# Where the softmax probabilities are scaled in a diffusion backbone step: on VectorE, or on ScalarE ahead of the recurrent roots

## What is computed

```python
s = jnp.einsum('bqgrd,bkgd->bgrqk', q, k) * (HEAD_DIM ** -0.5)
p = jax.nn.softmax(jnp.concatenate([s, sink_col], axis=-1), axis=-1)[..., :-1]
out = jnp.einsum('bgrqk,bkgd->bqgrd', p, v)
```

```python
u = jnp.sqrt(-jnp.expm1(2.0 * log_a)) * (i * xc)     # h = exp(log_a) * h + u
```

## Time and profile before

| | |
|---|---|
| median of 3 runs | 1509.36 us (1505.26 to 1509.89) |
| the profiled execution | 1510.04 us; its span, first to last instruction, is 1508.2 us |
| mean granted TensorE clock | 0.992 |
| busy, PE / DVE / ACT / POOL | 1448.1 / 1152.2 / 865.7 / 214.3 us |
| L1717, probabilities times reciprocal | 48 instructions, 285 to 423 ns |
| L1255, table loads and square roots | 16 loads of 1283 ns; 32 roots of 508 to 532 ns |

### The profile page before, as it was taken

One profiled execution on the slowest core, in us unless ns is written; L12 is line 12 of the kernel. 1 busy time (PEld: TensorE's weight loads), 2 busy tenths in 40 slices (PEclk: granted clock), 3 DMA queues, 4 the chain that ended last, 5 costly groups with the idle time before them and its releaser, 6 DMA issues.

```text
span 1508.2 us, 20056 instructions
## 1 busy us (share of the span) xinstructions
PE 1448.1 (96%) x7649; PEld 1223.4 (81%) x7649; DVE 1152.2 (76%) x1752; ACT 865.7 (57%) x1114; POOL 214.3 (14%) x252
## 2 busy tenths in 40 slices
PE   6999999999998999999999999999999899999996
PEld 3689888889876888888868988887998688888885
DVE  4447668886647999999864666888764799999986
ACT  1333467862226877788752345787322488887774
POOL 0100024400221110000140001342013111000002
PEclk9899999999999999999999999999999999999999
DMA  9456432216648999999864554213340999999993
GB/s 344 160 200 224 168 117 81 106 60 223 223 180 323 369 407 408 409 408 408 307 212 169 185 211 167 71 66 118 129 150 27 356 361 409 413 411 406 406 349 127
DMA packets 132422, 372.00 MB, mean 247 GB/s; under 512 B 9184, under 2 KB 12640, under 8 KB 132320
## 3 DMA queue, kind: packets, MB, share of 16 engines
q1 hardware_dynamic: 113728, 326.57, 57.6%
q0 software_dynamic: 10144, 24.13, 4.5%
q10 hardware_dynamic: 8448, 19.94, 3.4%
HBM read 350.66 MB, written 19.94 MB: 246 GB/s over the span
## 4 chain that ended last, share of the span: by engine, by line
PE 77%; DVE 9%; DMA 5%; ACT 4%; issue 4%; POOL 1%; SPq 0%; POOLq 0%; DVEq 0%; ACTq 0%
PE bank L581 29%; PE bank L931 20%; PE bank L937 10%; PE bank L591 2%; DMA ring<-in_w_ada 2%; PE bank L903 2%; PE bank L782 2%; PE bank L570 2%; PE bank L759 1%; DMA expert_rows<-gb 1%; PE bank L614 1%; DMA ring<-in_w_rnn_proj 1%; PE bank L696 1%; PE bank L691 1%; DVE ring_r L1635 1%
## 5 line engine op out<-in xcount | busy, mean ns | idle before, releaser
L2015 DVE TENSOR_TENSOR spot_low<-spot,piece_high 128x2048 fp32r<-128x2048 f32 x192 | 433.8, 2288 | 33.0 <-ACT piece_high L1353 31.4
L1353 ACT ACTIVATE piece_high<-spot 128x2048 fp32r<-128x2048 f32 x192 | 366.6, 1917 | 44.9 <-PE bank L937 42.8
L931 PE MATMUL bank<-piece_high,ga_r 128*128 128x512 f32 x768 | 308.7, 402 | 2.9 <-DVE spot_low L2015 1.6
L931 PE MATMUL bank<-spot_low,ga_r 128*128 128x512 f32 x768 | 301.7, 393 | 0.0
L581 PE MATMUL bank<-parts_r,gb_r 128*128 128x384 f32 x704 | 213.5, 340 | 4.0 <-ACT ga L1291 4.0
L937 PE MATMUL bank<-piece_high,ga_r 128*128 128x512 f32 x768 | 211.0, 396 | 3.7 <-DVE ga_r L2021 3.7
L581 PE MATMUL bank<-parts_r,ga_r 128*128 128x384 f32 x768 | 202.6, 345 | 0.0
L937 PEld LDWEIGHTS bank<-piece_high,ga_r 128*128 128x128 f32 x768 | 144.0, 188 | 39.3 <-DVE ga_r L2021 5.0
L931 PEld LDWEIGHTS bank<-piece_high,ga_r 128*128 128x128 f32 x768 | 144.3, 188 | 36.2 <-DVE spot_low L2015 2.7
L931 PEld LDWEIGHTS bank<-spot_low,ga_r 128*128 128x128 f32 x768 | 144.6, 188 | 30.6
L581 PEld LDWEIGHTS bank<-parts_r,ga_r 128*128 128x128 f32 x768 | 138.2, 188 | 5.9 <-issue 5.0
(11 more groups left out here) (365 smaller groups left out, 2519.6 us busy)
## 6 DMA issues: line engine op xcount, KB each, us to landing
spot<-in_w_gate_up SPq DMA_DIRECT2D x128, 1024.0 KB, 8.1
spot<-in_w_down SPq DMA_DIRECT2D x64, 1024.0 KB, 8.2
ring<-in_w_ada SPq DMA_DIRECT2D x24, 2048.0 KB, 8.0
ring<-in_w_in SPq DMA_DIRECT2D x22, 2048.0 KB, 8.0
expert_rows<-gb ACTq DMA_DIRECT2D x28, 512.0 KB, 7.2
ring<-in_w_attn_proj SPq DMA_DIRECT2D x4, 2048.0 KB, 8.2
ring<-in_w_rnn_proj SPq DMA_DIRECT2D x4, 2048.0 KB, 12.8
ring<-in_w_out SPq DMA_DIRECT2D x4, 2048.0 KB, 8.0
```

Source lines behind the costliest of these rows:

```text
L931: pe.matmul(out[n], high[:, 2 * q + k, :], w[:, k, n * 512:(n + 1) * 512], start=(q == 0 and k == 0 and i == 0), stop=False)
L1353: ac.activation(highs[p % HIGHS], spots[u], ACT.Copy).then_inc(S("piece_high"), 1)
L2015: ve.tensor_tensor(spots_low[u], spots[u], highs[p % HIGHS].bitcast(F32), ALU.subtract)\
```

## The change

The multiplication of the probabilities leaves VectorE and becomes an activation (`Copy` with a per-partition scale) on ScalarE, in place. VectorE signals `sum_ready` after the reciprocal; ScalarE waits for it, scales, and signals `probs_ready`, which TensorE waits for as before. In ScalarE's order the new step stands behind `att_copy(i - 2)` and ahead of the square roots of even rounds and of the copy out of the bank.

```diff
+                def probs(u):
+                    h, b = UNITS[u]
+                    w = P if b == 0 else LATK
+                    ac.wait_ge(S("sum_ready"), l * len(UNITS) + u + 1)
+                    ac.activation(pr[:, u % 2, 0:w], pr[:, u % 2, 0:w], ACT.Copy, scale=smx[:, u % 2, 5:6])\
+                        .then_inc(S("probs_ready"), 1)
+
...
                     if i >= 2:
                         att_copy(i - 2)
+                    probs(i)
                     if i > KT and i % 2 == 0:
                         lru_root(i - KT - 2)
                         lru_root(i - KT - 1)
...
                 def softmax_norm(u):
                     h, b = UNITS[u]
-                    w = P if b == 0 else LATK
                     ve.wait_ge(S("exp_done"), l * len(UNITS) + u + 1)
                     link(ve.tensor_tensor(smx[:, u % 2, 4:5], smx[:, u % 2, 2:3], smx[:, u % 2, 3:4], ALU.add))
-                    link(ve.reciprocal(smx[:, u % 2, 5:6], smx[:, u % 2, 4:5]))
-                    ve.tensor_scalar(pr[:, u % 2, 0:w], pr[:, u % 2, 0:w], smx[:, u % 2, 5:6], None, ALU.mult)\
-                        .then_inc(S("probs_ready"), 1)
+                    ve.reciprocal(smx[:, u % 2, 5:6], smx[:, u % 2, 4:5]).then_inc(S("sum_ready"), 1)
```

## The result

The kernel with the change takes 1521.47 us (median of 6 runs, 1515.61 to 1522.32) against 1509.62 us before (6 runs, 1505.26 to 1510.45): a ratio of 1.0079, with a 95% interval of 1.0063 to 1.0095. It is slower by 0.8%. The forecast was 1521.4.

A forecast was written before the change was run, and what follows sets the result against it. TensorE bounds the kernel; in the stage's ring of VectorE, ScalarE and TensorE, event order decides. Rounds 10 to 23 cost 5.2 us, early rounds 0.8: 6.0 a layer, 12.0 in all, 1521.4 us at the median; range 1519 to 1523.5.

The forecast's parts named there:

- The scaling's length: The new ScalarE activation: 0.61 us for 384 columns (bounds 0.51 and 0.70), 0.40 us for 128-column units.
- Even rounds: Rounds 10 to 22: reciprocal and scaling put off table load and roots, delaying L1728; seven rounds cost 6.56 us a layer.
- Odd rounds: Scaling covered by ScalarE's idle time; VectorE saves L1717's 0.34 us (0.20 for short units), 1.5 us a layer.
- Early rounds: From round 1 the scaling stands ahead of L1170 and the square VectorE's polynomial waits for: 0.8 us a layer.
- Where the delay goes: Behind the stage TensorE runs at its own pace, so the delay of 6.0 us a layer stays.
- Absorbed in part: Rival: losses in rounds 15 to 18 and 21 to 22 might be shed; 3.2 us a layer, 1515.8 us; chance 0.16.
- Relief wins: Rival: VectorE's shorter chain decides, ScalarE finds the reciprocal ready; not slower, 1508.3 or 1504.0 us; chance 0.12.
- Odd rounds bind: Rival: scaling of 1.1 us would exceed odd rounds' slack, 5.6 us a layer on top, some 1532 us; chance 0.04.

The follow-up runs named there:

- the experiment with the wait alone: Kernel before, scaling still on VectorE; only the wait for the reciprocal added on ScalarE, signalled by an empty VectorE instruction: 1512.2 us, one run.
- the experiment with the early rounds: Against the kernel before, the scaling goes to ScalarE only in rounds 0 to 8: 1509.3 us, one run.
- roots first: The changed kernel, but in even rounds the scaling stands behind the square roots: 1513.3 us, ratio 1.0029 to the kernel before.
- one column: Kernel before, scaling still on VectorE; ScalarE waits for the reciprocal, then copies one column at the change's place: 1519.6 us, one run.
- even rounds only: Against the kernel before, the scaling goes to ScalarE only in even rounds from 10 on: 1524.6 us, ratio 1.0102.

## Why the prediction was right

The forecast, slower by the roots' being put off, was right in mechanism and place; the time is within 0.1 us of the median, but that closeness is an accident: the change costs 10.1 us in the two stages, 10.5 without the pause of the kernel before, where 12.0 were forecast, and 1.1 us around the span, which the forecast did not have, fill most of the gap.

- **The scaling's length.** 0.61 and 0.40 us forecast; the medians are 0.617 for the long and 0.403 for the short units. An estimate from the Trainium skill's formula (ScalarE: Activation LUTs, What ACT_TABLE_LOAD costs), 0.60 and 0.39 us, comes within 0.02. The Trainium skill's rule (same page, Rules for kernel authors) that multiplications belong on VectorE holds here with all rounds moved (1.0079), but not round by round: with the odd ones alone moved the kernel is faster (0.9976).
- **Even rounds.** Forecast for the load: +0.84, +1.33, +0.72 by kind of round. Measured in the seven rounds of the first layer: 0.83, 1.31, 0.72, 0.84, 1.32, 0.72, 0.84. For L1728, now L1733: 0.82, 1.31, 0.72, 0.73, 1.32, 0.72, 0.72, 6.34 us in all against 6.56 forecast; in rounds 16 and 22 it had been waiting 0.1 us already, which I had not seen from round 10. Its waits are 1.20 to 2.06 us, a little above the 1.2 to 1.9 foretold.
- **Odd rounds: the step that was mis-sized.** I took 0.34 us for L1717. What VectorE saved is 0.46: with the multiplication went its wait for its own reciprocal, 0.20 us down to 0.08. The gain was "1.5 us"; from L1733 of one even round to the start of the next even one, VectorE is faster by 0.47, 0.48, 0.14, 0.47, 0.50 and 0.14 us in the second layer, 2.2 us. In the first layer 0.35 more came in round 10, where the kernel before had an idle 0.5 us behind the scan that is gone. So rounds 10 to 23 cost 3.9 and 4.2 us, not 5.2. The 0.35 is the pause described above, and no gain of the change: without it the first layer has 4.3.
- **Early rounds.** 0.8 us forecast; measured 0.8 up to the product of round 6, as the two waits show, and 0.2 more by that of round 7, 1.0.
- **Where the delay goes.** It stays: 10.5 us in the two stages without the pause, and 10.5 in the median of the spans.
- **The rivals.** "Absorbed in part" would have given 3.2 us a layer; TensorE has a wait behind every even round, so nothing was shed in rounds 15 to 18. "Relief wins" had the right gain and the wrong condition: as a kernel of its own, the odd rounds, it exists and is worth 1.6 and 1.7 us. "Odd rounds bind" did not occur; 0.49 us were left in round 11.

## What to carry to other kernels

When work moves between two engines that hand to each other in rounds, its price is set by what stands behind it in the receiving engine's order, not by the busy shares: here the same scaling gains 0.46 us where the receiver idles, and loses 0.7 to 1.3 where square roots wait behind it. Read each kind of round by itself and move only the rounds with a gap. And look in the giving engine's order for what stands ahead of the value handed over: moving one low part from between maximum and norm took back half of the loss.

## What the runs showed of the hardware

A table load starts before the wait of the activation that it serves is over (237.19 against a reciprocal that ends at 238.05, in the experiment with the wait alone). The trace has the load as an instruction of its own, ahead of the root, and it is the root that carries the semaphore. By an estimate from the load's 1.28 us, a wait directly ahead of a square root thus costs nothing up to about that length; 0.86 us is what was seen to be hidden. With a short activation between the wait and the root, 0.92 us of waiting put off the load in full. Otherwise a load is short and plain: in the changed kernel's round 12 it starts 0.02 us after the activation ahead of it ends, lasts 1.28, and the root starts 0.01 after it.

TensorE's granted clock can fall in the middle of a busy kernel, after a wait of 1.8 us. In the second layer of the experiment with the early rounds, a product that waited 1.79 us is followed by 3.5 us at a mean of 0.54 (columns as in the earlier trace rows):

```profile
920.15 0.99 PE L760 MATMUL bank<-pt,vl 128*128 128x128 f32 x4 [1.79 <-ACT qT L1235]
...
912.00:918.00 6.00, 6.00 (x39) 5.91 (x38) 3.73 (x10) 2.69 (x9) 0.00 (x0) 1.00 0.32 123
...
920.10:923.60 3.50, 3.45 (x15) 3.48 (x16) 2.09 (x4) 1.31 (x3) 1.42 (x3) 0.54 0.07 21
```

That is nearly the lower level, 1.2 GHz in place of 2.4, and it cost 1.4 us. The same followed waits of 1.81 us (roots first, clock 0.54 over 3.6 us), 1.85 (one column, 0.58 over 4 us) and 2.13 (even rounds only, 0.67 over 3 us), but not the changed kernel's own four of 1.78 and 1.79 us in its profiled execution. In all, the stages of the ten traces have 24 waits of 1.7 us or more, and a fall followed six of them; behind their shorter waits there was none. The executions of the kernel with the roots first range from 1507.9 us at a mean clock of 0.997 to 1522.8 at 0.988. So a wait of that length can cost more than itself, in some executions and not in others; that the wait is what brings the fall was not tested, and in the kernel with one column the time lost was made up in the next wait. That such stretches are behind the upper end of the change's own 1515.6 to 1522.3 us (mean clock 0.993 in the three longest, 0.996 in the shortest) is possible, and was not shown.
